# Norm of the last tokens moved from load_x and channel into the projections, whose first two blocks are split by tiles

## The reference

```python
def rmsnorm(x, g):
    y = x * lax.rsqrt(jnp.mean(x * x, axis=-1, keepdims=True) + EPS)
    return y * g

def split_proj(h, w_in):
    return jnp.split(h @ w_in, offs, axis=-1)      # a_h a_b a_c | b_q b_k b_v | c_q c_k c_v | c_qi c_ki c_wi | d_u d_v

# mixer C: relu(qi . ki) summed over 4 heads with weights wi, then the 256 best keys of each token
sc = jax.nn.relu(jnp.einsum('bthd,bsd->bths', qi, ki)); I = jnp.einsum('bth,bths->bts', wi, sc)

def finish(x, m, w_o, g_post_mix, g_pre_ffn, g_post_ffn, w_gate, w_up, w_down):
    x = x + rmsnorm(m @ w_o, g_post_mix)
    h = rmsnorm(x, g_pre_ffn)
    f = (jax.nn.silu(h @ w_gate) * (h @ w_up)) @ w_down
    return x + rmsnorm(f, g_post_ffn)
# a layer: m = mixer(rmsnorm(x, g_pre_mix[l]), ...); x = finish(x, m, ...)
```

## Time and profile before

| | us |
|---|---|
| median of 3 runs | 3196.37 (3194.83 to 3196.38) |
| the profiled execution, its own time | 3201.35 |
| its span, first to last instruction | 3199.6 |
| PE busy | 3045.2 (95%) |
| DVE busy | 1439.5 (45%) |
| ACT busy | 1045.9 (33%) |
| POOL busy | 737.7 (23%) |
| mean clock granted to PE | 0.978 |

### The profile page before, as it was taken

One profiled execution on the slowest core, in us unless ns is written; L12 is line 12 of the kernel. 1 busy time (PEld: TensorE's weight loads), 2 busy tenths in 40 slices (PEclk: granted clock), 3 DMA queues, 4 the chain that ended last, 5 costly groups with the idle time before them and its releaser, 6 DMA issues. The chain is left out here.

```text
span 3199.6 us, 48688 instructions
## 1 busy us (share of the span) xinstructions
PE 3045.2 (95%) x19762; PEld 2663.4 (83%) x19762; DVE 1439.5 (45%) x3314; ACT 1045.9 (33%) x2054; POOL 737.7 (23%) x528
## 2 busy tenths in 40 slices
PE   6999989889999999999979999899899999999998
PEld 5777756559899999999967777565698999999997
DVE  4468775547611111122554886755575111111115
ACT  2347625545311011111323666354542111110112
POOL 4002032305412121243200110413243121222131
PEclk8999989999999999999989999899899999999999
DMA  5120126643211111121321111356512111111131
GB/s 178 33 62 27 54 95 202 207 148 119 72 46 46 46 47 47 47 63 57 117 70 36 47 44 51 148 172 230 180 45 65 47 47 47 47 47 47 47 113 56
DMA packets 254072, 263.54 MB, mean 82 GB/s; under 512 B 24993, under 2 KB 224570, under 8 KB 253850
## 3 DMA queue, kind: packets, MB, share of 16 engines
q1 hardware_dynamic: 233370, 189.11, 18.9%
q0 software_dynamic: 20480, 71.32, 6.5%
HBM read 229.73 MB, written 30.65 MB: 81 GB/s over the span
## 5 line engine op out<-in xcount | busy, mean ns | idle before, releaser
L2037 PE MATMUL ps<-act_hi,w_hi 128*128 128x352 f32 x2112 | 685.7, 325 | 10.6 <-DVE act_lo L2495 10.3
L2037 PE MATMUL ps<-act_lo,w_hi 128*128 128x352 f32 x2112 | 679.0, 321 | 0.0
L2037 PE MATMUL ps<-act_hi,w_lo 128*128 128x352 f32 x2112 | 678.5, 321 | 0.0
L2416 POOL TENSOR_TENSOR w_lo<-w_raw,w_hi 128x1024 fp32r<-128x1024 f32 x132 | 322.0, 2442 | 1037.0 <-ACT w_hi L2254 1036.9
L677 PE MATMUL ps<-w_in_slots,hT 128*128 128x256 f32 (+1 forms) x2048 | 449.0, 375 | 0.0
L677 PEld LDWEIGHTS ps<-w_in_slots,hT 128*128 128x128 f32 x2048 | 374.9, 193 | 55.1 <-issue 6.8
L2037 PEld LDWEIGHTS ps<-act_hi,w_hi 128*128 128x128 f32 x2112 | 397.7, 188 | 15.7 <-issue 12.0
L2508 DVE TENSOR_TENSOR a_raw<-ps,silu 128x352 f32<-128x352 f32 x132 | 69.2, 524 | 750.6 <-PE ps L2037 746.5
L2037 PEld LDWEIGHTS ps<-act_lo,w_hi 128*128 128x128 f32 x2112 | 398.6, 189 | 0.5 <-issue 0.5
L2037 PEld LDWEIGHTS ps<-act_hi,w_lo 128*128 128x128 f32 x2112 | 397.5, 188 | 0.0
L2037 PE MATMUL ps<-a_hi,w_hi 128*128 128x352 f32 x1056 | 345.2, 327 | 0.0
(11 more groups left out here) (351 smaller groups left out, 4279.3 us busy)
## 6 DMA issues: line engine op xcount, KB each, us to landing
w_raw<-in_w_gate SPq DMA_DIRECT2D x44, 512.0 KB, 3.8
w_raw<-in_w_up SPq DMA_DIRECT2D x44, 512.0 KB, 3.8
w_raw<-in_w_down SPq DMA_DIRECT2D x44, 512.0 KB, 3.9
w_in_slots<-in_w_in SPq DMA_DIRECT2D x18, 1024.0 KB, 5.4
xpark<-xT SPq DMA_DIRECT2D x9, 1408.0 KB, 5.6
xT<-xpark SPq DMA_DIRECT2D x6, 1408.0 KB, 14.8
hT<-xpark SPq DMA_DIRECT2D x6, 1408.0 KB, 14.1
wo_raw<-in_w_o SPq DMA_DIRECT2D x16, 512.0 KB, 4.9
```

The source lines that it names most:

```text
L2037: ins = pe.matmul(bank(b), w, x, start=first and i == 0, stop=end and i == 2)
L2416: pool.tensor_tensor(w_lo[slot(j)][:, 0:K, :], w_raw[slot(j)][:, 0:K, :], w_hi[slot(j)][:, 0:K, :].bitcast(F32), ALU.subtract).then_inc(w_ ...
```

## The change

- In `mix_in` the first two blocks are walked in another order: IX tiles 0 to 4, CV tiles 0 to 4, IX tiles 5 to 8, CV tiles 5 to 8 (before: IX 0 to 8, CV 0 to 8). CHUNK_AT becomes 10, and with it SAMPLE_AT 20 and SPREAD_AT 31. The product of 32 rows for tile PT moves to tile 5 of these two blocks.
- The norm of the last tokens (`left`) leaves `load_x` (tokens 768 to 1055, 288 of them) and `channel` of layer 0 (third 2, 352 tokens) and goes into `mix_in`. In layer 1 DVE does `new_x_left` before anything else there. In both layers ACT squares after units 0, 1 and 2, PE sums after unit 4 (eight matmuls with the ones), ACT takes the root after unit 4, DVE inverts at unit 5 and writes `hT` at units 6 and 7. PE waits for all eight blocks of it before unit 10, ACT before its first relu.
- SP no longer waits at the end of `load_x` and `channel` for the writes to `xpark`. DVE waits for them in `mix_in` before it overwrites `xT`, at the index keys of tile 0 and of tile 5. In layer 1 SP writes the last third at the start of `mix_in`, once it is made.
- `gains` and the two `rstd` tiles get fixed places.

```diff
@@ load_x @@
-            sp.wait_ge(parked, 48)
-            total(2)
-                if p_ == 2:
-                    act.wait_ge(h_done, KC)
-            square(2)
-            root(2)
-            first_h(2)
@@ mix_in @@
-    units = []
-    for g in range(len(blocks)):
+    T0 = 5
+    units = [(g, n, 0) for tiles in (range(T0), range(T0, TILES)) for g in (IX, CV) for n in tiles]
+    for g in range(CQ, len(blocks)):
-    CHUNK_AT = TILES
+    CHUNK_AT = 2 * T0
+    left = slice(NEXT_LEFT if l else FIRST_LEFT, T)
+    NORM_AT = T0 - 1
 (SyncE)
+            if l:
+                sp.wait_ge(left_x, KC)
+                sp.dma_start(c.xpark.rearrange("p (k t) -> p k t", k=KC)[:, :, left], c.xT[:, :, left]).then_inc(c.x_last_parked, 16)
 (TensorE)
+                if i >= 2 * T0:
+                    pe.wait_ge(left_h, KC)
-                    if n == 0:
+                    if n == parts_at(g):
+                if i == NORM_AT:
+                    for k in range(KC):
+                        pe.wait_ge(left_sq, k + 1)
+                        ins = pe.matmul(ps[:, 7, 0:wide], c.ones[:, :], hT[:, k, left], start=(k == 0), stop=(k == KC - 1))
+                    ins.then_inc(left_sum, 1)
 (ScalarE)
+            def square_left(*ks):
+                for k in ks:
+                    if l:
+                        act.wait_ge(left_x, k + 1)
+                    act.activation(hT[:, k, left], c.xT[:, k, left], ACT.Square).then_inc(left_sq, 1)
+            def root_left():
+                act.wait_ge(left_sum, 1)
+                act.activation(rstd_x, ps[:, 7, 0:wide], ACT.Sqrt, bias=c.eps[:, 0:1], scale=1.0 / D).then_inc(left_root, 1)
+                if k == 0:
+                    act.wait_ge(left_h, KC)
+                if i < 3:
+                    square_left(*((0, 1, 2), (3, 4), (5, 6, 7))[i])
+                if i == NORM_AT:
+                    root_left()
 (VectorE)
+                if n == 0:
+                    dve.wait_ge(c.x_parked, 32)
+                if n == T0:
+                    dve.wait_ge(c.x_last_parked, 16)
+            def new_x_left():
+                dve.reciprocal(rstd_y, rstd_y).then_inc(left_inv, 1)
+                dve.wait_ge(left_inv, 1)
+                for k in range(KC):
+                    dve.scalar_tensor_tensor(out=c.xT[:, k, left], in0=c.xT[:, k, left], scalar=g_y[:, k:k + 1], in1=rstd_y,
+                                             op0=ALU.mult, op1=ALU.mult).then_inc(left_scaled, 1)
+                    dve.wait_ge(left_scaled, k + 1)
+                    dve.tensor_tensor(c.xT[:, k, left], c.xT[:, k, left], hT[:, k, left], ALU.add).then_inc(left_x, 1)
+            if l:
+                new_x_left()
+                if i == NORM_AT + 1:
+                    invert_left()
+                if i in (NORM_AT + 2, NORM_AT + 3):
+                    norm_left(*range(4 * (i - NORM_AT - 2), 4 * (i - NORM_AT - 1)))
@@ channel @@
-            sp.wait_ge(x2_done, 3 * KC)
-            sp.dma_start(third(xpark, 2), third(xT, 2)).then_inc(x2_parked, 16)
-            sp.wait_ge(x2_parked, 48)
+            sp.wait_ge(x1_in[2], 16)
-                take_x(2, *range(KC))
-            square_x2(2, *range(KC))
-            root_x(2)
-            invert_1(2)
-            new_x(2, *range(KC))
             next_h(1, 4, 5, 6, 7)
-            invert_2(2)
-            next_h(2, *range(KC))
```

More of the change, by code:

```diff
@@ L231, in load_x @@
     page_step, places, tables = sb("page_step", [P, 1]), sb("places", [1, DB * PAGES]), sb("tables", [1, DB * PAGES], I32)
[L232 removed]
+    g, sq, rstd = c.gains[:, 3, :], sb("first_sq", [P, W_SQ, 3 * P]), sb("first_rstd", [P, 2, 3 * P])
     assert nc.sbuf_base <= PAGES_AT
@@ L248, in _ @@
                 sp.dma_start(xt[:tok(n), n, :], src).then_inc(x_in[n], 16)
-            sp.dma_start(g[:, :], gain(io["g_pre_mix"], 0)).then_inc(g_in, 16)
+            sp.dma_start(g, gain(io["g_pre_mix"], 0)).then_inc(g_in, 16)
             load_columns(c, sp, 0, 0)
@@ L257, in _ @@
                 sp.wait_ge(kept_2, end)
-                sp.dma_start(c.xpark.rearrange("p (k t) -> p k t", k=KC)[:, :, at(p_)], xT[:, :, at(p_)]).then_inc(parked, 16)
+                sp.dma_start(c.xpark.rearrange("p (k t) -> p k t", k=KC)[:, :, at(p_)], xT[:, :, at(p_)]).then_inc(c.x_parked if p_ < 2 else c.x_last_parked, 16)
+            sp.wait_ge(g_in, 16)
             sp.wait_ge(rope_in, 32)
-            sp.wait_ge(parked, 48)
         @block.gpsimd
@@ L422, in early_buffers @@
     c.ki_sem, c.const_in = [sem(f"ki_in{ch}") for ch in range(PAST // 512)], sem("ix_const_in")
-    c.early_sems = [*c.w_in, *c.ki_sem, c.const_in]
+    c.x_parked, c.x_last_parked = sem("x_parked"), sem("x_last_parked")
+    c.early_sems = [*c.w_in, *c.ki_sem, c.const_in, c.x_parked, c.x_last_parked]
+    c.gains = c.nc.alloc_sbuf_tensor_at("gains", [P, 4, KC], F32, offset=GAINS_AT)
+    c.rstd_y, c.rstd_x = (c.nc.alloc_sbuf_tensor_at(n, [P, TH], F32, offset=c.m_at + 24576 + 4 * TH * i) for n, i in (("rstd_y", 3), ("rstd_x", 4)))
     c.wo_raw = c.nc.alloc_sbuf_tensor_at("wo_raw", [P, KC, D], F32, offset=c.m_at + 8 * KC * T + 4 * KC * D)
@@ L580, in mix_in @@
         done_by[i] = sum(e <= due for e in ends)
+    left = slice(NEXT_LEFT if l else FIRST_LEFT, T)
+    wide = left.stop - left.start
+    assert T0 * P <= FIRST_LEFT and T0 * P <= NEXT_LEFT
+    NORM_AT = T0 - 1
+    g_y, g_x, rstd_y, rstd_x = c.gains[:, 2, :], c.gains[:, 3, :], c.rstd_y[:, 0:wide], c.rstd_x[:, 0:wide]
+    left_inv, left_scaled, left_x, left_sq, left_sum, left_root, left_inv_x, left_h = (
+        s(f"left_{n}") for n in ("inv", "scaled", "x", "sq", "sum", "root", "inv_x", "h"))
     bank = [i % 2 if i < SPREAD_AT else (0, 1, 5, 6, 7)[(i - SPREAD_AT) % 5] for i in range(NU)]
@@ L587, in mix_in, with parts_at @@
     of_dve = [g in (AB, DU) or g in (A0, A1) and n == 1 for g, n, _ in units]
+    def parts_at(g):
+        return T0 if g in (IX, CV) else 0
     def wait_freed(eng, i):
@@ L1213, in background, with invert_left, norm_left @@
                     choose(j)
+            def new_x_left():
[6 more added lines that the diff above has]
+                    dve.tensor_tensor(c.xT[:, k, left], c.xT[:, k, left], hT[:, k, left], ALU.add).then_inc(left_x, 1)
+            def invert_left():
+                dve.wait_ge(left_root, 1)
+                dve.reciprocal(rstd_x, rstd_x).then_inc(left_inv_x, 1)
+                dve.wait_ge(left_inv_x, 1)
+            def norm_left(*ks):
+                for k in ks:
+                    dve.scalar_tensor_tensor(out=hT[:, k, left], in0=c.xT[:, k, left], scalar=g_x[:, k:k + 1], in1=rstd_x,
+                                             op0=ALU.mult, op1=ALU.mult).then_inc(left_h, 1)
+            if l:
+                new_x_left()
             dve.memset(mv[:, :, :], 1.0).then_inc(mv_set, 1)
@@ L1910, in channel @@
     sq, acc, rstd = place("mix_sq", at_scr + 8 * TH, [P, 2, TH]), place("mix_acc", at_scr + 16 * TH, [P, TH]), place("mix_rstd", at_scr + 20 * TH, [P, TH])
-    gains = place("gains", at_scr + 24 * TH + 128, [P, 4, KC])
+    gains = c.gains
+    assert at_scr + 24 * TH <= GAINS_AT
     def y(th, k):
@@ L1927, in channel @@
     a_raw = place("a_raw", over + 12 * T, [P, 2, TH])
-    assert over + 12 * T + 8 * TH <= PAGES_AT and max(at_tile) + 4 * T <= at_scr + 24 * TH + 128
-    sq2, acc2, rstd1, rstd2 = (place(n, c.m_at + 24576 + 4 * TH * i, [P, w, TH] if w > 1 else [P, TH])
-                               for n, i, w in (("down_sq", 0, 2), ("down_acc", 2, 1), ("down_rstd1", 3, 1), ("down_rstd2", 4, 1)))
+    assert over + 12 * T + 8 * TH <= PAGES_AT and max(at_tile) + 4 * T <= GAINS_AT
+    sq2, acc2 = place("down_sq", c.m_at + 24576, [P, 2, TH]), place("down_acc", c.m_at + 24576 + 8 * TH, [P, TH])
+    rstd1, rstd2 = c.rstd_y, c.rstd_x
     NYT, EARLY_Y = 8, 10
@@ L2023, in _ @@
                 sp.wait_ge(x2_done, KC * (th + 1))
-                sp.dma_start(third(xpark, th), third(xT, th)).then_inc(x2_parked, 16)
+                sp.dma_start(third(xpark, th), third(xT, th)).then_inc(c.x_parked, 16)
             sp.wait_ge(d_mm, 3 * KC)
@@ L2213, in _ @@
                 turn_y(*range(KC + 1, NYH))
-            else:
-                take_x(2, *range(KC))
         @block.scalar
```

11 lines of the change are left out of this document (6 added, 5 removed).

## The result

| | before | changed |
|---|---|---|
| median, same chip | 3196.82 (10 runs, 3189.27 to 3202.05) | 3204.86 (10 runs, 3203.09 to 3210.00) |
| profiled execution, its span | 3199.6 | 3202.9 |
| mean clock granted to PE | 0.978 | 0.978 |

The ratio is 1.0027 with an interval of 1.0017 to 1.0036: 8.6 us slower, between 5.4 and 11.5. The measured time lies inside its range, but near its upper end, and the likeliest case was "no difference", which this is not.

The account below looks back on a forecast made before the run. PE, busy 95% of the span, was taken to bound the kernel. Layer 0's +10.1 and layer 1's -8.2 gave +1.9 us on 3196.4, so 3198.3, with a range of 3188.5 to 3206.

Parts of the forecast that it names:

- start of layer 0: Before layer 0's first projection: removing the norm piece gains 0, as it stays hidden behind POOL's 32 gathers.
- start of layer 1: Border before layer 1: the norm's work on DVE, ACT and PE goes, so PE begins at 1611.1, not 1631.14: -20.0 us.
- sums: PE's eight new norm sums among the projections count in full: +4.0 us in layer 0, +4.8 in layer 1.
- first turn of layer 1: PE's turn of tile 0 before unit 4 comes 12.7 us after the start, behind DVE's new x: +0.9 us.
- rest of the norm: Layer 1's root, reciprocal and scalings finish near 1643, before PE reaches unit 10 near 1650: hidden, a cover of 7 us.
- units 10 to 20: IX tiles 5 to 7 carry scores and rope, DVE falls behind, banks free late: +1.3 us in each layer.
- end of `mix_in`: SPREAD_AT moves from 30 to 31, so the first mask follows unit 88 instead of 87: +4.8 us in each layer.
- Parking: Waits for the writes to xpark: already over before layer 0 starts, and moving them to DVE costs nothing.
- Rivals 2 to 5: Masks do not move, 3188.7, 8%; norm all hidden, about 3178, 4%; first-turn clock, 3203.1, 4%; layer 1 border unmoved, 3218, 3%.
- the forecast's own case: Whole kernel: no measurable difference ("same"), 3190.0 to 3202.8, with a chance of 66%.
- rival 1: Units 10 to 17: DVE and ACT lag, three waits of 1.58 us in each layer, +6.8, 3205.1; chance 15%.

Follow-up runs that it names:

- e1: The full change with its table of due steps counted from one unit earlier, against the kernel before: 3241.27, ratio 0.9987.
- e3: The change in layer 1 only, layer 0 keeping its old order, table and norm, against the kernel before: 3241.04, ratio 0.9987.
- e6: The change in layer 1 only, with its table counted from one unit earlier, against the kernel before: 3226.41, ratio 0.9965.
- e8: The kernel before with only the waits for x's parking moved from SP to DVE: 3238.54, ratio 1.0007, no difference.
- e4: The full change with no chunk of index scores on unit 13, later chunks one unit later, against the kernel before: 3244.76, ratio 0.9998.
- e5: The changed kernel again, unaltered, on another chip: 3242.50 against 3236.52 for the kernel before, ratio 1.0023.
- e9: The kernel before with POOL's 32 gathers moved from load_x to the head of its part of mix_in in layer 0: 3251.80, ratio 1.0017.

## Why the prediction was in range and yet missed its case

| step | predicted | measured |
|---|---|---|
| start of layer 0 | 0 | -0.15 (here; -5 to -6 on two other chips) |
| start of layer 1 | -20.0 | -20.07 |
| sums | +4.0, +4.8 | +3.9, +4.7 |
| first turn of layer 1 | +0.9, 12.7 us after the start | 12.3, wait 0.58 |
| rest of the norm | hidden | hidden, no wait before unit 10 |
| units 10 to 20 | +1.3 each layer | PE's waits there: +2.2 and +2.6 |
| waits elsewhere in the phase | no term | -0.2 and +0.7 (0.58 of it the first turn) |
| end of `mix_in` | +4.8 each layer | +4.66, +4.40 |
| clock behind the waits | not in the sum | +5.1, 0 |

**Right.** The border, the sums, the cover of the norm and above all the end of `mix_in`: that a shift of SPREAD_AT by one lets the masks go one unit later was read from the 1.21 us in the earlier trace rows and `done_by`, and e1, e3 and e6 each show it, at 4.4 to 4.8 us. Parking at nothing held (e8).

**The step that failed** is "Units 10 to 20: +1.3 in each layer". PE's waits in these units went from 2.88 to 5.12 us in layer 0 and from 3.20 to 5.83 in layer 1, so +2.2 and +2.6, and the mechanism was not the one named. The prediction looked for the narrow place on DVE and at units 10 to 12, which are short (2.39 us); there PE does not wait at all. The wait is at unit 13, whose product is 0.47 us, on ACT's relu of 2.06 us; the earlier trace rows had no row of a PT unit. The row that would have told it stands in the trace of before: PT's unit in CV carried a chunk and cost 1.30 us (PE and ACT):

```profile
113.42 0.62 PE L674 MATMUL ps<-sample_part,sum_heads 128*32 128x256 f32 x2
115.34 1.14 PE L707 MATMUL ps<-xT 32*128 32x512 f32 x8 [1.30 <-ACT vn L868]
...
113.56 1.64 ACT L868 ACTIVATE vn<-ps 128x384 f32<-128x384 f32 x4 [0.50 <-PE ps L707]
```

**The missing term** is the clock. The prediction weighed it in one place, the first turn of layer 1, where nothing happened, and counted every other wait at its own length. The 6.7 us between forecast (+1.9) and balance (+8.55) are the clock behind the waits in layer 0 (5.1), the waits of the whole phases (2.0 where 1.3 was put in layer 0, 3.4 where 1.3 and the first turn's 0.9 were put in layer 1: 1.9 together) and the 0.6 that stay open in layer 1, less 0.9 in small terms of the other sign. So the clock is the larger miss, though its mean over executions (2.8 us a phase, 5.6 in both) and not its split between the layers is what a forecast could have had.

**The rivals.** The first had a fitting time and the wrong cause: three new waits of 1.58 a layer for a lag of DVE. There are three waits in units 10 to 20 of layer 0 now (1.88, 1.66, 1.58), but two of them stood there before (1.30, 1.58), and e4 takes the new one away and leaves DVE's work. Rivals 2 to 5 (the masks do not move, all hidden, the clock at the first turn, the border does not move) did not occur.

**Luck.** The measured 3204.86 lies outside the forecast's own case and inside the range only because the range reached up to rival 1, whose cause is not the one at work. That it holds the result is luck.

**Not foreseen, and of no weight here:** that which engine ends `load_x` last depends on the chip. "Value 0" for the start of layer 0 is right for the chip of the profile and wrong by 5 to 6 us for two others.

## What to carry to other kernels

Before a list of units is reordered, look up everything that counts from a position in it: a table of due steps shifted by one cost nearly half of what the move gained (9.1 of 20.1 us), and one number mended it. Work hung on "each unit" is only hidden if that unit is long enough; find the shortest unit in the new order and put the longest attached step against it. And where PE is full, price a new wait of the size seen here higher than its length, since the low clock that may follow belongs to it.

## What the runs showed of the hardware

**The clock falls after short waits, though not after each.** In the traces of before, of the changed kernel and of e1 to e8, PE has 81 waits of 1.54 to 4.68 us inside the two phases. 37 of them were followed by a stretch at 0.50, most of them 1.7 us lost; over all 81 that is 0.8 us a wait. Of 46 waits between 0.39 and 1.30 us none was. The same wait in the same place (118.0 of e1 and 117.0 of e5, both 1.88 us) had it in one execution and not in another. The kernel before alone shows how far this draw reaches: of its runs on the chip of e5 to e8, 14 took 3228.59 to 3233.13 us at a mean clock of 0.974 to 0.977, and 15 took 3236.52 to 3247.13 us at 0.971 to 0.974. The Trainium skill (TensorE: Matmul & The Clock Gate, Why this matters for your kernels) warns of throughput drops by idle gaps between bursts; it speaks of longer gaps than nearly all of these, and by that line the waits here would be free of it. The measurement decides: about every second one was not.

**Indirect gathers can hold up the other engines.** On three of four chips PE, ACT and DVE stood for some 30 us while POOL issued 32 gathers, one every 1.27 us, and the standstill followed the gathers to another place (e9). On the chip of the first profiles they did not: ACT's first root, for one, came at 17.46 there and at 25.59 in e5, both with the changed kernel. The Trainium skill (GPSIMD Engine Reference, Specifications) has GpSimd and VectorE share SBUF interfaces; that alone does not say why ScalarE and TensorE stood too. Full DMA engines were not it: from 35 to 45 us of e5 their busy share is 0.19. What the engines lacked is not in these traces ("remote" and "issue" are all that the rows say), and why one chip is free of it stays open.
